# Moving half of the expert routing of a mixture-of-experts layer into the projection ahead of it

## What is computed

```python
xf = _rmsnorm(h, norm_g).reshape(t, d)
p_group = jax.nn.softmax(xr @ w_group + b_group, axis=-1)
g_sel = jnp.argmax(p_group, axis=-1)
e_logits = (xr @ w_expert + b_expert).reshape(t, N_GROUPS, EXPERTS_PER_GROUP)
e_logits = jnp.take_along_axis(e_logits, g_sel[:, None, None], axis=1)[:, 0]
top_p, top_i = lax.top_k(jax.nn.softmax(e_logits, axis=-1), TOP_K)
...
hid = jax.nn.silu(xb @ w_gate[e]) * (xb @ w_up[e])
return hid @ w_down[e]
```

## Time and profile before

| what | us |
|---|---|
| median of 3 runs (lowest to highest) | 2759.64 (2758.01 to 2762.12) |
| the profiled execution's own time | 2762.15 |
| its span | 2760.1 |
| TensorE busy in the span | 2645.4 |
| VectorE busy | 1850.2 |
| ScalarE busy | 1341.5 |
| GpSimd busy | 351.8 |

### The profile page before, as it was taken

One profiled execution on the slowest core, in us unless ns is written; L12 is line 12 of the kernel. 1 busy time (PEld: TensorE's weight loads), 2 busy tenths in 40 slices (PEclk: granted clock), 3 DMA queues, 4 the chain that ended last, 5 costly groups with the idle time before them and its releaser, 6 DMA issues.

```text
span 2760.1 us, 33359 instructions
## 1 busy us (share of the span) xinstructions
PE 2645.4 (96%) x13338; PEld 2115.9 (77%) x13338; DVE 1850.2 (67%) x2413; ACT 1341.5 (49%) x1917; POOL 351.8 (13%) x222
## 2 busy tenths in 40 slices
PE   7999899998999999999999999999999799999998
PEld 3577666776888888876888877878888688887877
DVE  5777565578776778795444247443344899999998
ACT  3541777434222333444452356344433577777775
POOL 1000460000000000000000000000000266333332
PEclk9999999999999999999999999999999899999999
DMA  9311210023443956623001130210024899999996
GB/s 329 123 62 47 104 47 1 20 103 120 154 151 136 343 209 241 232 94 135 3 31 46 46 123 1 92 61 1 1 72 166 331 367 392 386 383 382 381 375 250
DMA packets 149362, 451.25 MB, mean 163 GB/s; under 512 B 16762, under 2 KB 50840, under 8 KB 124624
## 3 DMA queue, kind: packets, MB, share of 16 engines
q1 hardware_dynamic: 132944, 419.33, 40.9%
q0 software_dynamic: 16256, 29.71, 3.0%
HBM read 411.21 MB, written 62.93 MB: 172 GB/s over the span
## 4 chain that ended last, share of the span: by engine, by line
PE 69%; DMA 12%; DVE 11%; ACT 6%; issue 2%; SPq 0%; POOL 0%; POOLq 0%; DVEq 0%; ACTq 0%
PE PS L181 64%; PE PS L192 5%; DMA MR<-in_w_e_up 4%; DMA MR<-in_w_e_gate 3%; DMA MR<-in_w_e_down 3%; DVE ML L4121 3%; ACT MH L4116 1%; PE PS L643 1%; DVE BIG L503 0%; ACT BIG L1104 0%; DVE ST L509 0%; DVE WOP L1999 0%; DMA BIG<-in_w_ada 0%; DVE XR L4250 0%; DMA BC<-in_w_ada 0%
## 5 line engine op out<-in xcount | busy, mean ns | idle before, releaser
L4121 DVE TENSOR_TENSOR ML<-MR,MH 128x2048 fp32r<-128x2048 f32 x144 | 329.5, 2300 | 29.3 <-ACT MH L4116 28.8
L181 PE MATMUL PS<-MH,MX 128*128 128x512 f32 x1024 | 323.2, 397 | 11.8 <-DVE ML L4121 9.2
L4116 ACT CAST MH<-MR 128x2048 fp32r<-128x2048 f32 x144 | 275.3, 1914 | 91.1 <-DMA MR<-in_w_e_up 42.1
L181 PE MATMUL PS<-BIG 128*64 128x128 f32 (+12 forms) x1616 | 244.0, 349 | 15.9 <-DVE BIG L4443 5.0
L181 PEld LDWEIGHTS PS<-MH,MX 128*128 128x128 f32 x1024 | 190.4, 190 | 57.2 <-DVE ML L4121 16.8
L181 PEld LDWEIGHTS PS<-BIG 128*64 128x64 f32 (+5 forms) x1616 | 144.6, 164 | 77.2 <-issue 51.5
L181 PE MATMUL PS<-ML,MX 128*128 128x512 f32 x512 | 200.9, 392 | 0.0
L181 PE MATMUL PS<-WOP,T4R 128*128 128x512 f32 x672 | 155.0, 389 | 1.4 <-DVE WOP L2266 1.4
L181 PE MATMUL PS<-T1R,T2R 128*128 128x512 f32 x672 | 154.6, 389 | 0.0
L192 PE MATMUL PS<-CT,BIG 128*128 128x128 f32 (+3 forms) x1016 | 137.3, 274 | 15.9 <-ACT BIG L1332 5.8
L192 PEld LDWEIGHTS PS<-CT,BIG 128*128 128x128 f32 (+3 forms) x1016 | 116.0, 138 | 46.3 <-issue 14.7
(11 more groups left out here) (641 smaller groups left out, 6037.9 us busy)
## 6 DMA issues: line engine op xcount, KB each, us to landing
MR<-in_w_e_gate SPq DMA_DIRECT2D x50, 1024.0 KB, 19.3
MR<-in_w_e_up SPq DMA_DIRECT2D x48, 1024.0 KB, 20.0
MR<-in_w_e_down SPq DMA_DIRECT2D x46, 1024.0 KB, 19.3
BIG<-in_w_ff SPq DMA_DIRECT2D x32, 1024.0 KB, 7.2
BIG<-fz SPq DMA_DIRECT2D x28, 1024.0 KB, 4.9
fz<-BIG SPq DMA_DIRECT2D x48, 512.0 KB, 2.7
XR<-in_w_e_down SPq DMA_DIRECT2D x18, 1024.0 KB, 18.6
BC<-in_w_ada SPq DMA_DIRECT2D x32, 512.0 KB, 3.5
```

The lines of the kernel that those rows point to most:

```text
L181: ins = pe.matmul(o, l, r, start=(start and n == 0), stop=(stop and n == len(pairs) - 1), skip_group_check=True)
L4116: act.copy(cut_at(MH, i), raw(i)).then_inc(e.w_hi.up(), 1)
L4121: dve.tensor_tensor(cut_at(ML, i), raw(i), cut_at(MH, i).bitcast(F32), ALU.subtract).then_inc(e.w_lo.up(), 1)
```

## The change

Router work moves one tile closer behind the projection: `co_pe_after(t)` now does the logits of tile t-2 and the turn of tile t-1, and ScalarE copies tile t-1. Behind the projection there remain the logits of tiles 6 and 7 and the turn of tile 7.

`dve_choose(0, 4)` is called after VectorE's work on tile 5, amid the projection, and `dve_choose(4, 8)` alone stands at the end. Ranking is split likewise: a new `dve_rank(0)` for tiles 0 to 3 stands after VectorE's work on tile 6, with a new `pe_before_early` on TensorE (4 small bf16 matmuls) after the projection of tile 6, and `dve_rank(1)` at the end. The tables that the choice needs (`dve_setup`) are made after tile 4. The two operations `ge` and `dd` (gates) move behind `dve_rank(1)`. The scratch of the routing moves to places that are free by then (`CSN`, `CT`); the definitions move ahead of `co_pe_after` otherwise unchanged.

```diff
+        def pe_before_early():
+            P.wait_ge(*mem_of[1])
+            mm(PRE[0], [(SUB, MMB[:, 0:128].rearrange("p (t n) -> p t n", t=4))])
+            for s_ in range(3):
+                ins = mm(PRE[0][:, s_ + 1:4, :], [(ONEB, member(s_, 3 - s_))], start=False)
+            ins.then_inc(pre_mm.up(), 1)
...
+        def dve_rank(e):
...
+            dve.tensor_scalar(ids[:, :, :, 0:32], oh, C("tok")[:, 0:1], None, ALU.mult).then_inc(vs.up(), 1)
...
+            V.wait_ge(*(mem_mm if e else pre_mm)[1])
+            dve.tensor_tensor(part, oh, PRE[e].unsqueeze(1).to_broadcast([128, 2, 4, 32]), ALU.mult).then_inc(vs.up(), 1)
+            step().tensor_reduce(ranks, part, AX, ALU.add).then_inc(vs.up(), 1)
...
+            for c in range(2):
+                a = 8 * (1 - e) + 4 * c
+                dve.tensor_tensor(PH[:, a:a + 4, :], io.unsqueeze(1).to_broadcast([128, 4, 128]),
...
         def co_pe_after(t):
-            if t >= 3:
-                logits(t - 3)
             if t >= 2:
-                turn_tile(t - 2)
+                logits(t - 2)
+            if t >= 1:
+                turn_tile(t - 1)
+            if t == 6:
+                pe_before_early()
...
             act_rms(t, ue_sq, ue_ms, ue_std)
-            if t >= 2:
-                act_turn_tile(t - 2)
+            if t >= 1:
+                act_turn_tile(t - 1)
...
+            if t == 4:
+                dve_setup()
+            if t == 5:
+                dve_choose(0, 4, 4)
+            if t == 6:
+                dve_rank(0)
...
-        logits(5)
-        turn_tile(6)
-        act_turn_tile(6)
         logits(6)
...
         def dve_route():
...
-            dve_choose(0, 6, 6)
-            dve_choose(6, 8, 8)
+            dve_choose(4, 8, 8)
+            dve_rank(1)
```

More of the change, by code:

```diff
@@ L3960, in co_dve_lead, with wk_, bt, halfs @@
                 dve_values(7)
+        W9 = slot(10)
+        wat = [1024]
+        def wk_(n):
+            a = wat[0]
+            wat[0] += n
+            assert wat[0] <= 4096
+            return W9[:, a:a + n]
+        def bt(ap, n):
+            return ap.unsqueeze(2).to_broadcast([128, ap.shape[1], n])
+        def halfs(ap, k):
+            return ap.bitcast(BF16).rearrange("p (k n) -> p k n", k=k)
+        io = C("io")
+        thr = C("thr")
+        BX = [128, 16, 32]
+        ge_in, ge_ok, dd_in, dd_ok = by_dve("ge_in"), by_act("ge_ok"), by_dve("dd_in"), by_act("dd_ok")
@@ new lines, in program @@
+        eq = CSN[:, 288:544].rearrange("p (t n) -> p t n", t=8)
+        ge, eq4 = (CSN[:, a:a + 32].rearrange("p (t n) -> p t n", t=8) for a in (544, 576))
+        gm, gi, m1, i1, m2, i2, dd, T16 = (CSN[:, a:a + 8] for a in range(608, 672, 8))
+        rk = CSN[:, 672:688]
+        OH = CT[:, 640:1152].rearrange("p (k n) -> p k n", k=16)
+        tabs = CT[:, 1152:1408]
+        EM = CT[:, 1408:1664].rearrange("p (t n) -> p t n", t=8)
+        assert CONSTS["caus"][0] <= 640 and CONSTS["su"][0] >= 1664
@@ new lines, in program @@
+        prod = wk_(512).rearrange("p (k n) -> p k n", k=16)
+        MMB, SUB, ONEB = (tabs[:, a:b].bitcast(BF16) for a, b in ((0, 128), (128, 192), (192, 256)))
+        EQ2 = tabs[:, 0:240].rearrange("p (k n) -> p k n", k=16)
+        TOT, IDF = wk_(32), wk_(32)
+        RBV = [halfs(CT[:, 304:560], 8), halfs(wk_(256), 8)]
+        PH = halfs(bc(2), 16)
+        RBG = halfs(bc(3)[:, 0:768], 16)
+        GT = bc(3)[:, 768:784]
+        GTR = bc(3)[:, 784:800]
+        GTP = [bc(3)[:, 800 + 8 * i:808 + 8 * i].bitcast(BF16) for i in range(3)]
@@ new lines, in program, with step, gstep, dve_first_max @@
+        PH2 = PH
+        SC_ = [bc(3)[:, 832 + 48 * i:880 + 48 * i] for i in range(2)]
+        os_, qq, cq, blk, rkm = bc(3)[:, 928:960], wk_(16), wk_(16), wk_(16), wk_(16)
+        RB2 = halfs(bc(3)[:, 0:600], 16)
+        def step():
+            V.wait_ge(*vs.last)
+            return dve
+        def gstep():
+            G.wait_ge(*gs.last)
+            return gps
+        def dve_first_max(x, n, m_, i_, e_):
+            step().tensor_reduce(m_, x, AX, ALU.max).then_inc(vs.up(), 1)
+            step().tensor_tensor(e_, x, bt(m_, n), ALU.is_equal).then_inc(vs.up(), 1)
+            step().scalar_tensor_tensor(out=e_, in0=e_, scalar=-64.0, in1=io[:, 64:64 + n].unsqueeze(1).to_broadcast(
+                [128, x.shape[1], n]), op0=ALU.mult, op1=ALU.add).then_inc(vs.up(), 1)
+            step().tensor_reduce(i_, e_, AX, ALU.min).then_inc(vs.up(), 1)
@@ L4370, in program @@
[L4370 to L4384, removed]
@@ L4499, in pe_gate_slots @@
             P.wait_ge(*gr_of[3])
[L4500 removed]
+            mm(PS[:, 7, 64:160], [(PH[:, ph_at(k), :], RBG[:, k, :]) for k in range(16)]).then_inc(gs_mm.up(), 1)
         def dve_gate_slots():
```

160 lines of the change are left out of this document (68 added, 92 removed).

## The result

The changed kernel takes 2767.28 us, the median of 16 runs (2762.68 to 2771.22). The kernel before has a median of 2761.53 over 16 runs, among them the three from which the prediction started, whose median (2759.64) lay 1.9 us lower. One of the 16 was a slow run of 4933.76 us, which the ratio leaves out. The ratio of changed kernel to kernel before is 1.0020 with a 95% interval of 1.0013 to 1.0027: 5.5 us slower, 3.6 to 7.5, worked out on 2761 us. The profiled execution has a span of 2766.3 us and an own time of 2768.43.

A forecast was written before the change was run, and what follows sets the result against it. The landing of the first gather was taken to bound the kernel. Landing 3.1 us later plus 0.8 for the clock made 3.9, added to 2759.64 for a median of 2763.5 us; range 2758.5 to 2768.

The forecast's parts named there:

- What bounds the stage: End of routing: the first gather's landing releases experts' matmuls and remaining weights; its shift reaches the kernel's end in full.
- E moves: First slot behind the projection's last TensorE matmul: 5.3 us later, from wait 2.45, extra logits-and-turn pair 2.53, early matmuls 0.35.
- The clock: TensorE behind the new wait: granted clock may fall to 0.50, costing 0 or 1.6 us; half, 0.8, taken.
- The last logits, the choice, the ranks: Behind the projection: choice of tiles 4 to 7 takes 5.5 us, ranks 4.2; index table 0.7 us later, at 2149.8.
- Amid the projection: VectorE's early routing is hidden in its gaps: tile 6 late by 1.2 us, tile 7 on time by some 0.6.
- The gather: First gather of token rows, now beside weights: takes 7.9 us instead of 5.5, landing 3.1 us later, at 2158.6.
- The 8.8: Alternative gather time if DMA engines alternate its packets with the weights': 8.8 us, kernel 0.9 us above the forecast.
- `xz` as not last: Tile 7's rows transfer, landing moved from 2143.3 to 2148.6, isn't the last thing the first gather waits for.
- The sum: Whole kernel: landing 3.1 us later plus 0.8 for the clock, 3.9 us slower, median 2763.5.
- the gather would take its usual 10.8 beside weights: Rival at the first gather: full competition, landing 5.9 us later, 7.5 with fallen clock, giving 2767.1; chance 0.25.
- E would stay: Rival: projection's end unmoved and router work hidden, gather landing 2.3 us earlier, 2757.3; chance 0.09.
- the early choice would not fit: Rival on VectorE: choice amid the projection 1 to 2 us longer, delaying tile 7's sum, 2764.5 to 2765.5; chance 0.08.

The follow-up runs named there:

- e11: e4 with only four weight pieces, not eight, ahead of the first gather; −0.3 us against the kernel before (ratio 0.9999).
- e7: Kernel before, with the first half of the one-hot rows written four more times so the index table comes later; +5.5 us against the kernel before.
- e2: Changed kernel with ten unused matmuls filling TensorE's wait ahead of the turn of tile 0; +2.8 us against the kernel before.
- e6: Changed kernel with six weight pieces, not eight, ahead of the first gather; +1.4 us against the kernel before.
- E1: Changed kernel with the turn of tile 0 back at its old place, 12 matmuls later; +0.6 us against the kernel before.
- e3: Kernel before with only the router work moved one tile closer, choice and ranks left whole at the end; +6.6 us against the kernel before.
- e8: Changed kernel run again, unaltered; +4.7 us against the kernel before.
- e5: Kernel before with the start of the weight stream also waiting for tile 7's norm; +2.2 us against the kernel before.
- e9: e4 with only six weight pieces, not eight, ahead of the first gather; −2.8 us against the kernel before (ratio 0.9990).
- e10: Kernel before with only six weight pieces ahead of the first gather, routing untouched; −1.4 us against the kernel before.
- e4: Changed kernel with TensorE's and ScalarE's order of before and the choice by two tiles in VectorE's gaps; −1.4 us against the kernel before.

## Why the prediction was right, and where its sum was short

**What bounds the stage: right.** The landing of the first gather decides, and a shift of it passes through to the end. In the twelve profiles of the table other than e11's the end comes 603.7 to 607.0 behind the landing, and e7 shows it with a delay made for the purpose. "Change" lies within the interval of every measured time, for e11 (−2.5, measured −0.3) only just. Since the distance from landing to end scatters by 3.3 us between profiles, a shift of 1 or 2 us can't be followed to the end in one of them.

**E moves: right, and nearly in size.** Predicted 2.45 for the wait, 2.53 for the pair, 0.35 for the early matmuls, 5.3 in all. Measured with the clock at full (e2, e6): 45.77 − 40.34 = 5.4. E1 isolates the last two (2.87), e3 the first two (5.2). The first wait is 2.34.

**The clock: its price right, the half a toss.** The prediction put half of 0 or 1.6 into the sum. Among the four profiles with this wait of 2.34 to 2.35, the clock fell in two (after and e8, E − N 47.4) and stayed in two (e6 and, without the early matmuls, e3). The price when it falls is 47.4 − 45.77 = 1.6. Four profiles don't give its chance, and what decides between the two is open; that the half served the sum is luck as much as reading.

**The last logits, the choice, the ranks: right.** The choice starts 8.21 behind E (predicted 8.24), takes 5.66 (5.5), the ranks 3.92 (4.2), and the table is ready at E + 17.8 (E + 17.9). Amid the projection, tile 6's sum starts 1.35 us after the slot behind that tile's last matmul (2125.12 to 2126.47), where tile 7's takes 0.20 (2133.43 to 2133.63): 1.15 late (predicted 1.2), and ahead of tile 7's VectorE waits for TensorE again, 0.64 us (0.6).

**The gather: the mis-sized term, and a picture of it that the traces don't bear out.** I took 7.9, the shortest I saw in a full stream, because the company would end after six us. Measured 8.5 and 8.2 in the changed kernel, 8.5, 8.4 and 9.6 in e1, e5 and e2. The company did end about when it should: the DMA engines are full in the whole window from 2152 to 2156 and, by windows of 1 us behind it, until 2159 (0.93 to 1.05), then 0.63 until the landing. But up to 2158 the gather had hardly begun: 0.03 MB of it had moved.

The gather's packets have a queue of their own (q0 on the page, the weights q1), and windows of 0.1 us show when they move. In the seven profiles whose weights are through by 2.6 us behind the gather's issue (before, e3, e6, e7, e9, e10, e11), its first packet comes 2.9 us behind the issue. In the five whose weights run on for 5.6 to 7.0 us (after, e1, e2, e5, e8) it comes 5.3 to 5.5 behind, and in e4, with 4.7, 4.3. From the first packet to the landing it is 2.5 to 3.2 us in all of them but e2, whose weights run on longest (4.2). In the changed kernel not one packet of the gather is recorded between the end of its preparation (2154.44) and 2157.6, while 179 of the weights are. So some 2.5 of the 3 us that the gather loses are a later start of its packets, and only the rest, mostly in e2, is a slower transfer. What holds the first packet back while the weights run stays open.

By the Trainium skill ("DMA: Bandwidth & Descriptors", section on queues, rings and completion order) an engine takes packets from its rings in turn. Once both queues move, the trace agrees: in e2, from 5.5 to 7.0 us behind the issue, 59 packets of the gather run beside 61 of the weights. The 8.8 that the prediction worked out from that in a sentence apart is nearer to these runs than my 7.9, but by luck: it has the gather share from the start and move at half its speed, and the traces have it start late and then move nearly as fast as alone.

**`xz` as not last: right by a hair.** I had it 2.1 us ahead of the issue, with the transfer of before (12.7 us). It took 13.7 in the changed kernel, landing at 2151.17, hardly ahead of the table (2151.22), and 14.2 in e8, where it was the last by half a microsecond. So the margin of that step was mis-sized too, though it cost at most 0.5.

**The sum.** Put together with measured terms: E − N up by 5.4 and half of 1.6, the landing behind E earlier by 29.0 − 27.2 = 1.8, that is 4.4, against the 3.9 predicted and the 5.5 and 4.7 measured. 0.5 is the gather. The other 0.3 to 1.1 lie inside the intervals and stay open. (By its own terms the prediction's 3.1 is 3.0: 2158.6 − 2155.56.) Of the 3.8 between the predicted median (2763.5) and the measured one, 1.9 come from the three runs of before, whose median lay low. That the measured median lies inside the predicted range owes something to luck: the forecast itself went to some 5 later, and the top of the range, 2768, came from a rival that did not happen, the gather of 10.8 with the fallen clock.

**The rivals.** That the gather would take its usual 10.8 beside weights did not come: 8.2 to 9.6. That E would stay did not come either; e4 does keep E, and shows what that rival said of itself: the gather then meets the weights (6.8) and the gain stays below what can be measured. That the early choice would not fit did not come: VectorE was in time for tile 7. Of the two further rivals formed for the runs, the split choice costs nothing (e1 against e3: the split shortens the tail behind E from 29.0 to 27.2), and the weight stream does not decide with eight or six pieces ahead of the gather, but has a part in it with four.

So why did so much early routing bring nothing? It shortens the tail from E to the issue of the gather by 4.8 us (23.43 to 18.67). But it was bought with 5.4 to 7.0 us on E, and 3 of the 4.8 went to a gather that now starts ahead of the stream's end.

## What to carry to other kernels

Moving work ahead on an engine that runs without a gap does not hide it: it moves the end of that stage by its whole length, by the wait for an input that is not there yet, and perhaps by a fallen clock, so look first where the operand is ready and put the work behind that (e1 gave back 4.9 of 5.5 us, 4.2 by its profile, by 12 matmuls' difference). Where a dependent transfer is brought forward, look at what is on the DMA engines at its new time, and let prefetches that aren't needed at once wait for it; here six pieces ahead of it were right, four too few. Use gaps of the idle engine without touching the full one: only the forms of this change that did so (e4, e9, e11) had the gather land earlier than before, and e9's time alone is below the kernel before by more than the noise.

## What the runs showed of the hardware

- The same wait of TensorE (2.34 to 2.35 us, nearly the same code around it) is followed by a granted clock of 0.50 in some executions and of 1.00 in others, with 11 against 15 or 16 matmuls in a window of 2.5 us behind the turn's start. When it falls it costs 1.6 us once.
- The first gather takes 5.5 to 6.1 us by itself, 6.8 where the weights end midway, and 8.2 to 9.6 where they run on for 5.6 to 7.0 us behind its issue. Most of the difference is a later start: its first packet comes 2.9 us behind the issue without weights and 5.3 to 5.5 beside them, and the landing follows 2.5 to 3.2 us after that (4.2 in one).
- The start of one stage deep in the kernel differs by up to 5 us between executions whose code ahead of it is the same (N at 2086.07 and 2081.67 in the two profiles of the changed kernel, at 2081.11 in e4 and 2086.34 in e11), while distances inside it repeat to 0.02 us (E − N 40.33 to 40.35 in seven kernels). A change of a few microseconds is read from distances, not from two spans.
